# Moving the stationary buffers of the large products to 32 bytes past a 128-byte line

## The chip, the cores and the metric

The kernel runs on one core of one Trainium2 chip. The metric is device time in microseconds. Three runs of the kernel before took 1442.66, 1443.53 and 1445.46 us; the median is 1443.53.

## What is computed

A two-layer encoder trunk over 256 tokens of width 1024, all in float32:

```
h = x
hn = rms_norm(h, norm_mix[0]);  h += fourier_mixer(hn, w_in, w_out)        # h @ w_in, 2-D DFT by 4 groups, real part, @ w_out
hn = rms_norm(h, norm_ffn[0]);  h += (silu(hn @ w_gate) * (hn @ w_up)) @ w_down      # width 2816
hn = rms_norm(h, norm_mix[1]);  h += neighbourhood_attention(hn, w_qkv, rpb, w_o)    # 16 heads, 4 x 64 grid
hn = rms_norm(h, norm_ffn[1]);  h += moe_swiglu(hn, ...)                   # 8 experts of width 3584, the best 2 by token
out = rms_norm(h, final_norm)
```

Every expert's three matrices (1024 x 3584 twice, 3584 x 1024) are used, whatever the routing is, so all weights are read once: 423 MB in all.

## The kernel before

**The weight stream.** All large weight matrices are cut into pieces of 128 partitions x 2048 float32, 1 MB each: 4 row tiles x 512 columns for gate, up and projections, 2 row tiles x 1024 columns for down. SyncE loads them in order into seven buffers, `raw0` to `raw6` (L293). Each piece is then split in two, since a product in full float32 would be slow: ScalarE copies it to `w_hi` in the type float32r (L365), and VectorE writes the rest, `w_lo = raw - w_hi` (L624). There are three `w_hi` and three `w_lo` buffers. TensorE waits for `lo_made`, uses the piece, and its last matmul raises `piece_used`, on which ScalarE waits before it refills that buffer three pieces later. VectorE's `lo_made` frees the raw buffer for the next load.

**The large products.** The activations are split in the same way. The helper `three` (L995 to L997) issues three matmuls for one 128 x 128 block of activations and one row tile of weights:

```
nc.tensor.matmul(out_, xh, wh, start=start, stop=False)   # L995
nc.tensor.matmul(out_, xh, wl, start=False, stop=False)   # L996
return nc.tensor.matmul(out_, xl, wh, start=False, stop=stop)   # L997
```

The first operand, `xh` or `xl`, is the stationary one: 128 columns, loaded anew by an LDWEIGHTS ahead of each matmul. The second, `wh` or `wl`, is the moving one, 512 columns wide in nearly all cases. The stationary operand is `act_hi`/`act_lo` in the dense projections (w_in, w_out, gate, up, qkv, w_o; two blocks of 128 tokens), `hidT_hi`/`hidT_lo` in the down products of the dense layer and of the experts, and `xg_hi`/`xg_lo` in the gate and up products of the experts, whose tokens (at most 128) are gathered by a product with a selection matrix `sel` (L1299) and scattered back by `selT` (L1396, L1397). The Fourier mixer is made of products too: `u` by the table `dft` along the tokens (512 wide), then `dft` by `pt` along the channels (256 wide). In the profile's names the moving operand stands first: `bank_Y<-w_hi,hidT_hi` is moving `w_hi`, stationary `hidT_hi`.

**The order.** It is written out by hand, engine by engine. In an expert TensorE does, for each of 7 steps of 512 hidden columns, the gate product (2 pieces, 24 matmuls), the transposes of the step before (L1333), the up product (24) and the down product of the step before (24). Near the end of an expert come the gather for the next one and its transposes (L1310), then the last down products and the scatter. The 8 experts are a hardware loop with the same addresses each time.

**Where the buffers lie.** `sb(name, shape, dt)` in `trunk` allocates on-chip buffers one behind the other; each starts at the next multiple of 32 bytes. The order is `raw0` to `raw6`, `h`, `hn`, `gains`, `mask`, `act_hi`, `act_lo`, `ident`, some small ones, `silu_g`, `hid`, `hidT_hi`, `hidT_lo`, `arena`, `w_hi`, `w_lo`. The arena is one stretch in which four layouts lie over each other, one for each phase (Fourier, attention, experts, and the bias tables); `dft`, `u`, `pt`, `qT`, `kT`, `v`, `xg_hi`, `xg_lo`, `y_hi`, `y_lo`, `sel` and `selT` are in it. Three pads of 32 bytes, `pad_h`, `pad_g` and `pad_w`, stand ahead of `h`, `silu_g` and `w_hi`.

Of the kernel before, what the change touches and what calls it, by code (L numbers as in the profile page):

```python
# [26 lines left out]
P = 128  # L27
# [14 lines left out]
BANK = 512  # L42
PIECE = 2048
RAW = 7
SPLIT = 3
KH = PIECE // BANK
KROW = PIECE // D
# [58 lines left out]
PER_EXPERT = len(EXPERT)  # L106
assert PER_EXPERT % RAW == 0 and PER_EXPERT % SPLIT == 0


def expert_source(ewg, ewu, ewd, e, j):  # L110

    kind, c, half = EXPERT[j]
    v = {"gate": ewg, "up": ewu, "down": ewd}[kind][0].rearrange("e (k p) n -> p (e k) n", p=P)
    if kind == "down":
        return v[:, bass.ds(e * (FFE // P) + (BANK // P * c + KROW * half), KROW), :], KROW, D
    return v[:, bass.ds(e * KD + KH * half, KH), BANK * c:BANK * (c + 1)], KH, BANK


def trunk(nc, x, norm_mix, norm_ffn, w_in, w_out, w_qkv, w_o, ffg, ffu, ffd, router_w, router_b,
# [7 lines left out]
    N0 = len(dense)  # L127
    dense += [expert_source(ewg, ewu, ewd, 0, j) for j in range(SPLIT)]
    N1 = len(dense)


    def sb(name, shape, dt=f32):
        return nc.alloc_sbuf_tensor(name, shape, dt)

    raw = [sb(f"raw{i}", [P, PIECE]) for i in range(RAW)]
    sb("pad_h", [P, 8])
    h = sb("h", [P, NB, D])
    hn = sb("hn", [P, NB, D])
    gains = sb("gains", [P, 4, KD])
    mask = sb("mask", [P, GRID])  # L140
    act_hi = sb("act_hi", [P, KD, S], f32r)
    act_lo = sb("act_lo", [P, KD, S], f32r)
    ident = sb("ident", [P, P])
    sumsq = sb("sumsq", [P, 5, NB])
    rstd = sb("rstd", [P, 5, NB])
    half_power = sb("half_power", [P, NB])
    sb("pad_g", [P, 8])
    silu_g = [sb(f"silu_g{i}", [P, BANK]) for i in range(2)]
    hid = [sb(f"hid{i}", [P, BANK]) for i in range(2)]
    hidT_start = -(-nc.sbuf_base // 32) * 32  # L150
# [3 lines left out]
    def width_of(shape):  # L154

        return -(-4 * int(np.prod(shape[1:])) // 32) * 32

    def layout(entries, off):

        made = {}  # L160
        for name, shape, dt in entries:
            made[name] = nc.alloc_sbuf_tensor_at(name, shape, dt, offset=off)
            off += width_of(shape)
        return made
# [16 lines left out]
             ("gap", [P, NB], f32), ("ratio", [P, NB], f32), ("den", [P, NB], f32), ("g1", [P, NB], f32),  # L181
             ("g2", [P, NB], f32), ("weight", [P, NB, NE], f32), ("slot", [P, NB, 2 * NE], f32),
             ("most", [P, 1], f32), ("flag", [P, 1], i32)]
    arena_start = -(-nc.sbuf_base // 32) * 32
    sizes = [sum(width_of(shape) for _, shape, _ in l) for l in (fourier_l, attn_l, moe_l, bias_l + bias_l)]
    sb("arena", [P, max(sizes) // 4])
    sb("pad_w", [P, 8])
    w_hi = [sb(f"w_hi{i}", [P, PIECE], f32r) for i in range(SPLIT)]
    w_lo = [sb(f"w_lo{i}", [P, PIECE], f32r) for i in range(SPLIT)]
    fo, mo = (layout(l, arena_start) for l in (fourier_l, moe_l))  # L190
# [18 lines left out]
    def sem(name):  # L209
        return nc.alloc_semaphore(name)  # L210


    raw_in = [sem(f"raw_in{i}") for i in range(RAW)]
    hi_made, lo_made, piece_used, part_made = sem("hi_made"), sem("lo_made"), sem("piece_used"), sem("part_made")
# [35 lines left out]
    def piece(j, E, back=0):  # L250

        return j + 1 - back if E is None else E * PER_EXPERT + (N0 + j + 1 - back)

    def slot_of(j, E, n):
        return (j if E is None else N0 + j) % n

    def has_before(j, E, back):

        return E is not None or j >= back
# [28 lines left out]
    def _(sp):  # L288
        def load(j, E, src, tiles):
            s = slot_of(j, E, RAW)  # L290
            if has_before(j, E, RAW):
                sp.wait_ge(lo_made, piece(j, E, RAW))
            sp.dma_start(raw[s][:].rearrange("p (k n) -> p k n", k=tiles), src).then_inc(raw_in[s], 16)  # L293
# [9 lines left out]
        def expert_loads(E):  # L303

            for j in range(SPLIT, PER_EXPERT + SPLIT):
                e = E % NE if j < PER_EXPERT else (E + 1) % NE
# [49 lines left out]
    def _(act):  # L356
        made = [0]

        def split_hi(j, E):
            s, w = slot_of(j, E, RAW), slot_of(j, E, SPLIT)  # L360
            rounds = 16 * (j // RAW + 1) if E is None else 16 * ((N0 + j) // RAW + 1) + E * (16 * PER_EXPERT // RAW)
            act.wait_ge(raw_in[s], rounds)
            if has_before(j, E, SPLIT):
                act.wait_ge(piece_used, piece(j, E, SPLIT))
            nc.scalar.activation(w_hi[w][:], raw[s][:], ACT.Copy).then_inc(hi_made, 1)  # L365
# [1095 lines left out]
```

## Time and profile before

| | |
|---|---|
| median of three runs | 1443.53 us (1442.66 to 1445.46) |
| the profiled execution | 1442.99 us; span of its instructions 1441.1 us |
| TensorE matmul busy | 1398.6 us, 97% of the span, 6483 matmuls |
| VectorE busy | 1137.7 us, 79% |
| ScalarE busy | 944.7 us, 66% |
| GpSimd busy | 20.7 us, 1% |
| DMA | 423.16 MB, mean 294 GB/s |
| granted TensorE clock | 0.993 of full speed, mean over the span |

The dense part takes the first 335 us, attention and routing the next 90, and the eight experts some 1000 us, 125 us each. Matmuls are pipelined, so the records of two neighbours overlap: one of 512 columns is recorded with 0.39 us, while the next begins about 0.23 us after it. The distance between the starts tells the rate, the recorded duration doesn't.

### The profile page before, as it was taken

The page shows a single profiled execution, that of the slowest core. Times are in us where ns is not written, and L with a number is a line of the kernel's source. Part 1 is how long each engine was busy: PE and PEld are TensorE (multiplying, and loading weights), DVE is VectorE, ACT ScalarE, POOL GpSimd, SP SyncE. Part 2 cuts the span into 40 slices and gives each one's busy share as a digit, 9 for nine tenths or more (in the row PEclk, how much of TensorE's full clock was granted, in tenths as well). Part 3 has the DMA queues.
Part 4 walks back from the last instruction along what each step waited for, and adds up shares of the span by engine and source line. Part 5 has one row for each costly group of instructions (what it writes and reads, how often), then busy time and mean ns, then how long its engine had stood idle before and what let it go on. Part 6 is the DMA issues. An engine that isn't in the chain of part 4 may idle for free.

```text
span 1441.1 us, 17938 instructions
## 1 busy us (share of the span) xinstructions
PE 1398.6 (97%) x6483; PEld 1146.4 (80%) x6483; DVE 1137.7 (79%) x814; ACT 944.7 (66%) x773; POOL 20.7 (1%) x26
## 2 busy tenths in 40 slices
PE   6999999999979999999999999999999999999995
PEld 5888888787868887887888788788878878887884
DVE  5455666655578889888888988898898888889887
ACT  5354344445657777777777777777777777777775
POOL 0000000000120000000000000000000000000001
PEclk9999999999999999999999999999999999999998
DMA  9358775562149998998999899899989989999992
GB/s 356 106 170 225 215 207 176 175 205 88 59 135 340 371 377 304 373 369 311 367 378 355 318 370 369 315 362 365 370 307 381 363 321 372 357 353 332 368 375 85
DMA packets 192979, 423.16 MB, mean 294 GB/s; under 512 B 19184, under 2 KB 21360, under 8 KB 192944
## 3 DMA queue, kind: packets, MB, share of 16 engines
q1 hardware_dynamic: 179728, 418.15, 80.7%
q10 hardware_dynamic: 12784, 3.26, 1.6%
q0 software_dynamic: 432, 1.28, 0.3%
q8 instruction: 22, 0.36, 0.1%
q14 instruction: 13, 0.11, 0.0%
HBM read 421.61 MB, written 1.05 MB: 293 GB/s over the span
## 4 chain that ended last, share of the span: by engine, by line
PE 91%; DVE 3%; ACT 2%; issue 2%; POOL 0%; DMA 0%; ACTq 0%; DVEq 0%; POOLq 0%
PE bank_G L995 10%; PE bank_G L997 10%; PE bank_G L996 10%; PE bank_U L995 9%; PE bank_U L997 9%; PE bank_U L996 9%; PE bank_Y L995 8%; PE bank_Y L997 8%; PE bank_Y L996 8%; PE bank_T L1333 2%; DVE w_lo L624 1%; PE bank_G L1230 1%; PE bank_T L995 1%; PE bank_T L996 1%; PE bank_T L997 1%
## 5 line engine op out<-in xcount | busy, mean ns | idle before, releaser
L624 DVE TENSOR_TENSOR w_lo<-raw,w_hi 128x2048 fp32r<-128x2048 f32 x394 | 896.4, 2290 | 210.5 <-ACT w_hi L365 209.7
L365 ACT ACTIVATE w_hi<-raw 128x2048 fp32r<-128x2048 f32 x394 | 754.6, 1918 | 290.7 <-PE bank_U L997 93.3
L995 PE MATMUL bank_Y<-w_hi,hidT_hi 128*128 128x512 f32 x492 | 194.3, 395 | 0.0
L997 PE MATMUL bank_Y<-w_hi,hidT_lo 128*128 128x512 f32 x492 | 192.5, 391 | 0.0
L996 PE MATMUL bank_Y<-w_lo,hidT_hi 128*128 128x512 f32 x492 | 192.1, 390 | 0.0
L995 PE MATMUL bank_U<-w_hi,xg_hi 128*128 128x512 f32 x448 | 181.3, 405 | 0.5
L995 PE MATMUL bank_G<-w_hi,xg_hi 128*128 128x512 f32 x448 | 177.3, 396 | 1.4 <-DVE w_lo L624 0.5
L997 PE MATMUL bank_G<-w_hi,xg_lo 128*128 128x512 f32 x448 | 175.8, 392 | 0.0
L997 PE MATMUL bank_U<-w_hi,xg_lo 128*128 128x512 f32 x448 | 175.7, 392 | 0.0
L996 PE MATMUL bank_U<-w_lo,xg_hi 128*128 128x512 f32 x448 | 174.2, 389 | 0.0
L996 PE MATMUL bank_G<-w_lo,xg_hi 128*128 128x512 f32 x448 | 174.1, 389 | 0.0
L997 PEld LDWEIGHTS bank_Y<-w_hi,hidT_lo 128*128 128x128 f32 x492 | 92.4, 188 | 21.3
L996 PEld LDWEIGHTS bank_Y<-w_lo,hidT_hi 128*128 128x128 f32 x492 | 92.4, 188 | 19.8
L995 PEld LDWEIGHTS bank_Y<-w_hi,hidT_hi 128*128 128x128 f32 x492 | 92.5, 188 | 19.2
L995 PEld LDWEIGHTS bank_G<-w_hi,xg_hi 128*128 128x128 f32 x448 | 84.2, 188 | 21.7 <-DVE w_lo L624 4.7
L997 PEld LDWEIGHTS bank_G<-w_hi,xg_lo 128*128 128x128 f32 x448 | 84.1, 188 | 19.6
L997 PEld LDWEIGHTS bank_U<-w_hi,xg_lo 128*128 128x128 f32 x448 | 84.1, 188 | 19.5
L996 PEld LDWEIGHTS bank_G<-w_lo,xg_hi 128*128 128x128 f32 x448 | 84.1, 188 | 18.4
L995 PEld LDWEIGHTS bank_U<-w_hi,xg_hi 128*128 128x128 f32 x448 | 84.3, 188 | 17.2 <-DVE w_lo L624 2.1
L996 PEld LDWEIGHTS bank_U<-w_lo,xg_hi 128*128 128x128 f32 x448 | 84.3, 188 | 16.5
L995 PE MATMUL bank_G<-w_hi,act_hi 128*128 128x512 f32 (+1 forms) x176 | 68.2, 388 | 6.6 <-DVE w_lo L632 4.2
L995 PE MATMUL bank_U<-w_hi,act_hi 128*128 128x512 f32 (+1 forms) x176 | 67.7, 385 | 0.0
(262 smaller groups left out, 1482.8 us busy)
## 6 DMA issues: line engine op xcount, KB each, us to landing
raw<-in_expert_w_gate SPq DMA_DIRECT2D x114, 1024.0 KB, 7.2
raw<-in_expert_w_up SPq DMA_DIRECT2D x113, 1024.0 KB, 7.2
raw<-in_expert_w_down SPq DMA_DIRECT2D x112, 1024.0 KB, 6.8
raw<-in_nat_w_qkv SPq DMA_DIRECT2D x12, 1024.0 KB, 5.0
raw<-in_ffn_w_gate SPq DMA_DIRECT2D x11, 1024.0 KB, 8.8
raw<-in_ffn_w_up SPq DMA_DIRECT2D x11, 1024.0 KB, 5.2
raw<-in_ffn_w_down SPq DMA_DIRECT2D x11, 1024.0 KB, 5.5
raw<-in_fourier_w_in SPq DMA_DIRECT2D x4, 1024.0 KB, 11.3
```

The source lines that it names most:

```text
L365: nc.scalar.activation(w_hi[w][:], raw[s][:], ACT.Copy).then_inc(hi_made, 1)
L624: nc.vector.tensor_tensor(w_lo[w][:], raw[s][:], w_hi[w][:].bitcast(f32), ALU.subtract).then_inc(lo_made, 1)
L995: nc.tensor.matmul(out_, xh, wh, start=start, stop=False)
L996: nc.tensor.matmul(out_, xh, wl, start=False, stop=False)
L997: return nc.tensor.matmul(out_, xl, wh, start=False, stop=stop)
L1230: last = nc.tensor.matmul(G[i % 2][:, S * n:S * (n + 1)], att["qT"][p0:p0 + HD, m, P * b:P * (b + 1)], att["kT"][p0:p0 + HD, m, :], start= ...
L1333: last = nc.tensor.transpose(T[c % 2][:, P * k:P * (k + 1)], hid[c % 2][:, P * k:P * (k + 1)], ident[:])
```

## The change

The three fixed pads become computed ones, and two more are asked for. `past_line(name, 32)` allocates just what is missing for the next buffer to start 32 bytes past a multiple of 128, and nothing where it does so already. Nothing else is changed: no instruction, no wait, no order.

```diff
 RAW = 7
+LINE = 128
...
+    def past_line(name, bytes_past):
+        base = -(-nc.sbuf_base // 32) * 32
+        if (bytes_past - base) % LINE:
+            sb(name, [P, (bytes_past - base) % LINE // 4])
+
     raw = [sb(f"raw{i}", [P, PIECE]) for i in range(RAW)]
-    sb("pad_h", [P, 8])
+    past_line("pad_h", 32)
     h = sb("h", [P, NB, D])
...
     mask = sb("mask", [P, GRID])
+    past_line("pad_act", 32)
     act_hi = sb("act_hi", [P, KD, S], f32r)
...
-    sb("pad_g", [P, 8])
+    past_line("pad_g", 32)
     silu_g = [sb(f"silu_g{i}", [P, BANK]) for i in range(2)]
...
+    past_line("pad_a", 32)
     arena_start = -(-nc.sbuf_base // 32) * 32
...
     sb("arena", [P, max(sizes) // 4])
-    sb("pad_w", [P, 8])
+    past_line("pad_w", 32)
     w_hi = [sb(f"w_hi{i}", [P, PIECE], f32r) for i in range(SPLIT)]
```

## Rows read from the trace of the kernel before

**Rows 1.** The page, parts 1 and 4: TensorE's busy time; the chain by engine.
```profile
PE 1398.6 (97%) x6483; PEld 1146.4 (80%) x6483; DVE 1137.7 (79%) x814; ACT 944.7 (66%) x773; POOL 20.7 (1%) x26
PE 91%; DVE 3%; ACT 2%; issue 2%; POOL 0%; DMA 0%; ACTq 0%; DVEq 0%; POOLq 0%
```

**Rows 2.** By stage: us, busy PE, PEld, DVE, ACT, POOL, clock, DMA share, GB/s.
```profile
85.00:150.00 65.00, 65.00 (x297) 53.90 (x296) 36.84 (x28) 31.70 (x28) 0.92 (x2) 1.00 0.71 202
...
675.00:800.00 125.00, 124.26 (x560) 101.36 (x559) 109.84 (x69) 92.39 (x64) 0.00 (x0) 1.00 0.97 353
```

**Rows 3.** TensorE's timeline, dense up product: start us, us; first and last of 48.
```profile
96.63 0.39 PE L995 MATMUL bank_U<-w_hi,act_hi 128*128 128x512 f32 x1
...
107.28 0.39 PE L997 MATMUL bank_U<-w_hi,act_lo 128*128 128x512 f32 x1
```

**Rows 4.** TensorE's timeline, dense down product: first and last of 48.
```profile
130.17 0.39 PE L995 MATMUL bank_Y<-w_hi,hidT_hi 128*128 128x512 f32 x1
...
140.93 0.39 PE L997 MATMUL bank_T<-w_hi,hidT_lo 128*128 128x512 f32 x1
```

**Rows 5.** TensorE's timeline, expert: down product, then gate; first and last of 48.
```profile
574.61 0.39 PE L995 MATMUL bank_Y<-w_hi,hidT_hi 128*128 128x512 f32 x1
...
585.37 0.40 PE L997 MATMUL bank_G<-w_hi,xg_lo 128*128 128x512 f32 x1
```

**Rows 6.** Groups by line and form: xcount, busy us, mean ns, idle before.
```profile
L995 PE MATMUL bank_Y<-w_hi,hidT_hi 128*128 128x512 f32 x492 | 194.3, 395 | 0.0
L995 PE MATMUL bank_U<-w_hi,xg_hi 128*128 128x512 f32 x448 | 181.3, 405 | 0.5
L995 PE MATMUL bank_G<-w_hi,xg_hi 128*128 128x512 f32 x448 | 177.3, 396 | 1.4 <-DVE w_lo L624 0.5 <-DVE xg_lo L643 0.2
...
L995 PE MATMUL bank_G<-w_hi,act_hi 128*128 128x512 f32 x160 | 63.7, 398 | 6.6 <-DVE w_lo L632 4.2 <-DVE act_lo L647 1.4 <-DVE act_lo L643 0.9
...
L995 PE MATMUL bank_T<-w_hi,hidT_hi 128*128 128x512 f32 x40 | 15.8, 394 | 0.0
```

**Rows 7.** TensorE's timeline, expert, just behind the gather: first and last of 12.
```profile
661.09 0.40 PE L995 MATMUL bank_Y<-w_hi,hidT_hi 128*128 128x512 f32 x1
...
663.65 0.40 PE L997 MATMUL bank_Y<-w_hi,hidT_lo 128*128 128x512 f32 x1
```

**Rows 8.** The chain in order of time, start of an expert: start us, us, what.
```profile
682.07 1.10 issue
...
687.95 0.50 PE bank_G L995
```

**Rows 9.** TensorE's timeline, Fourier products: a run of 9, and a run of 24.
```profile
38.80 0.39 PE L995 MATMUL bank_T<-dft_hi,u_hi 128*128 128x512 f32 x1
...
40.61 0.39 PE L997 MATMUL bank_T<-dft_hi,u_lo 128*128 128x512 f32 x1
...
43.96 0.28 PE L995 MATMUL bank_Y<-pt_hi,dft_hi 128*128 128x256 f32 x1
...
46.72 0.28 PE L997 MATMUL bank_Y<-pt_hi,dft_lo 128*128 128x256 f32 x1
```

**Rows 10.** Groups by line and form, VectorE, the 128x512 rests.
```profile
L643 DVE TENSOR_TENSOR hidT_lo<-bank_T,hidT_hi 128x512 fp32r<-128x512 f32 x66 | 44.7, 683 | 3.6 <-ACT hidT_hi L459 3.6
...
L643 DVE TENSOR_TENSOR act_lo<-bank_G,act_hi 128x512 fp32r<-128x512 f32 x2 | 1.3, 686 | 2.2 <-ACT act_hi L491 2.2
```

**Rows 11.** Timelines of ScalarE and VectorE: one piece's split in an expert.
```profile
699.71 1.92 ACT L365 ACTIVATE w_hi<-raw 128x2048 fp32r<-128x2048 f32 x1 [0.82 <-PE bank_U L997]
...
701.73 2.29 DVE L624 TENSOR_TENSOR w_lo<-raw,w_hi 128x2048 fp32r<-128x2048 f32 x1
```

**Rows 12.** The tile raw: from the issue of a load to its landing.
```profile
DMA to landing us min/median/max: 4.7/7.0/16.7
```

**Rows 13.** TensorE's timeline: the first matmul of two experts, one after the other.
```profile
676.12 0.40 PE L995 MATMUL bank_G<-w_hi,xg_hi 128*128 128x512 f32 x1
...
801.01 0.40 PE L995 MATMUL bank_G<-w_hi,xg_hi 128*128 128x512 f32 x1
```

## The prediction

> **What bounds the kernel now.** I read the page's busy shares and the chain of waits first, then the table by stage, then the waits, and last the timeline of TensorE, row by row. The page has TensorE busy 97% of the span, and 91% of the chain that ended last is TensorE [rows 1]. The table by stage says the same of both halves: busy 65.00 of 65 us in a dense stretch and 124.26 of 125 us in an expert, at a granted clock of 1.00, which is the 2.4 GHz level [rows 2]. So the span is a count of matmuls times the distance between two starts; a busy time can't show that distance, since matmuls overlap in the records. It must be read as (last start minus first start) over the number of steps in a stretch without a gap.
>
> The kernel holds a natural experiment on exactly this. By the sizes in the program (a buffer starts at the next multiple of 32 bytes; the first is at 8320) act_hi and act_lo, w_hi and w_lo begin 32 bytes past a 128-byte line, while everything from silu_g to the arena's end begins 96 bytes past one: hidT_hi, hidT_lo, xg_hi, xg_lo, the gather's and scatter's operands, the Fourier operands.
> - Stationary act (32) with moving w (32): 48 matmuls in a row start between 96.63 and 107.28 us [rows 3], so 10.65/47 = 226.6 ns apart.
> - Stationary hidT (96), same moving buffers, a few us later at a like DMA load: 48 matmuls between 130.17 and 140.93 us [rows 4], 10.76/47 = 228.9 ns.
> - Expert phase, hidT and then xg (both 96): 48 matmuls between 574.61 and 585.37 us [rows 5], again 228.9 ns.
>
> The difference is 2.3 ns a matmul, it sets in with the first matmul on hidT without any wait between, and it is the same for two bank pairs, two tile families and two DMA loads. What those slow stretches have in common, and the fast one hasn't, is the place of the stationary operand.
>
> **The change, part by part.** No instruction is added or removed. Only addresses move.
> 1. pad_h: raw ends on a multiple of 128, so the computed pad is the same 32 bytes. The new pad_act comes out as none, since act_hi is at 32 already. h, hn, act, ident: nothing moves, cost 0.
> 2. pad_g grows from 32 to 96 bytes: silu_g, hid, hidT_hi, hidT_lo and the whole arena (xg, y, sel, selT, dft, u, pt, q, k, v) move up 64 bytes, from 96 to 32 past the line. This is the part that can pay.
> 3. pad_a comes out as none; pad_w grows by 64 bytes to 96, so w_hi and w_lo move up 128 bytes in all: still 32 past a 128-byte line.
>
> The value of part 2. The w-matmuls on hidT and xg are three for each row of line 995: 492 + 448 + 448 + 40 = 1428 rows, so 4284 matmuls [rows 6] (another four such rows are left out). If they step at the pace of rows 3, they save 4284 × 2.34 ns = 10.0 us. Bounds: nothing, if the place isn't the cause; and a little more, since after the gather of each expert a stretch runs at (663.65 - 661.09)/11 = 232.7 ns [rows 7] on the same hidT, and it might come down as well (some 20 matmuls in each of 8 experts, 6 ns: 1.0 us).
>
> What is not on the path. In each expert, right after the first gate product, PE waits for a piece that ACT was late with: between 682.07 and 687.95 us the chain runs through the table load, silu, w_hi and w_lo, not through the 24 matmuls of the first up product, which are issued meanwhile [rows 8]. Those 24 finish 0.06 us earlier and PE waits that much longer: 8 × 24 × 2.3 ns = 0.4 us, taken off.
>
> Gather (72), scatter (64) and Fourier token products (48) also move from 96 to 32, both operands at once. Their starts are unsteady, near 232 ns; at 226.6 the 184 would save 0.9 us, at unchanged pace nothing. I take 0, as they follow stalls or other shapes, and keep 0.9 for the range. The 256-wide products of the channel transform ran 24 matmuls from 43.96 to 46.72 us, 120 ns apart [rows 9]; the dense 256-wide ones on act are alike, so nothing is expected there. The 128-wide transposes, scores and p·v products have no pair to compare and are put at nothing either way.
>
> ACT and DVE also read and write moved tiles. Each 128x512 rest on DVE took 683 ns for hidT_lo at 96 and 686 ns for act_lo at 32 [rows 10]: no difference, and the large split (2290 ns) keeps its places in the line. They follow PE in any case.
>
> What could be late next. A piece takes 12 matmuls. ACT begins to refill a freed buffer at 699.71 us and DVE ends its half at 701.73 + 2.29 = 704.02 [rows 11]; PE wants it two pieces after it was freed, at about 705.2. At 2.72 us a piece instead of 2.75 that margin of 1.2 us loses 0.06. The loads come 4.7 to 16.7 us after issue, with a median of 7.0 [rows 12], seven buffers turn over in about 19 us, and no wait of ACT on a load appears among the long waits. The DMA would have to move 353 × 124.9/123.7 = 356 GB/s [rows 2], and single slices of this trace already show up to 381. So the gain should come through whole: 10.0 - 0.4 = 9.6 us.
>
> The sum is made against the profiled execution, 1442.99 us (span 1441.1): it becomes 1433.4. The median of the runs shown is 0.5 above it, so I forecast 1434.0. An expert, from 676.12 to 801.01 us now 124.89 us [rows 13], should take 124.89 - 480 × 0.00234 = 123.8.
>
> **A rule that speaks against it.** The trace shows a cost at 96 that isn't there at 32 [rows 3, 4]. The Trainium skill, page "SBUF — State Buffer", section "Specifications (TRN2)", gives 16-byte cachelines and a penalty for each crossing. Both 32 and 96 are whole such lines, and all rows here are contiguous, so by that rule the place costs nothing and the sum is 0. The measured rows decide for the larger step, but they don't prove that the step is 128 bytes.
>
> **The rivals.**
> - *It isn't the place in the line.* act differs from hidT and xg in other ways: act_lo lies 8192 bytes behind act_hi, the others 4096; act is read every 1024 bytes along k, the others every 512. For this: the Fourier token products, both operands at 96, ran from 38.80 to 40.61 us in 8 steps of 226.3 ns [rows 9], the fast pace, and their u_lo lies 8192 behind u_hi; and hidT itself ran at two paces [rows 5, 7]. Against: later Fourier products with the same tiles were slow. Then nothing changes: 1443.5 us.
> - *It is the distance between the stationary and the moving operand.* That was 64 in the slow stretches and 0 in act's and in the Fourier ones; after the change it is 0 throughout. Same time as the forecast; it belongs to it, and explains rows 9 better.
> - *The line that counts is 256 bytes or more.* w_hi0 goes from 169504 to 169632, that is from byte 32 to byte 160 of 256, and act stays at 32. If a moving operand there costs what the worst steady stretch shows, 232.7 ns [rows 7], then 4284 × 3.8 ns + 1056 × 6.1 ns (act: 352 rows of line 995, 160 of them in bank G [rows 6], as many in U, 16 each in Y and T) = 16.3 + 6.4 = 22.7 us more: 1466. In its mild form only act falls back to 228.9: 1056 × 2.3 ns = 2.4 us, 1446. It decides as soon as the dense act stretches aren't at 226.6 any more. Against: nothing in the trace distinguishes 32 from 160 of 256.
> - *Another engine takes over.* By the margins above PE's pace would have to fall by 0.1 us a piece and more before ACT and DVE bind; if half the gain were lost so, 1439.
>
> **How the numbers follow.** About 0.2%, 2.9 us, is what a measurement of this kernel can tell from no change. Forecast: 0.72, own range 1431.5 to 1437 (upper end: one third of the matmuls keep their pace; lower end: gather, scatter, Fourier and the 232.7 stretches come down too). Nothing: 0.15. Half lost: 0.04. 256-byte line, mild 0.03, full 0.06. Faster is 0.72 + 0.04 = 0.76, same 0.15 + 0.03 = 0.18, slower 0.06. The range reaches from 1431.5 up past the no-change case, to 1444.5.
>
> **What would show it.** Right: in the timeline the products on hidT and xg start 226.6 ns apart as act's do; an expert takes 123.8 us; w_lo stays at 2290 ns and w_hi at 1918; the wait for w_lo after each expert's first up product grows by 0.06 us. Wrong: 228.9 ns still there with everything at 32 (then another property of these tiles is the cause), act's stretches no longer at 226.6 (then 256 counts), or the new pace there and the expert still at 124.9 (then PE is not what sets the end).

## The result, and the profile after

The changed kernel takes 1463.89 us (median of 4 runs, 1462.22 to 1464.13), the kernel before, run beside it, 1443.22 us (median of 4). The ratio is 1.0138, 95% interval 1.0124 to 1.0152: slower by 20.7 us, where 9.5 us less had been forecast. The time lies near the rival "the line that counts is 256 bytes or more" in its full form (1466), which had been given a chance of 0.06.

The page of the changed kernel, parts 1, 4 and 5, answers to [rows 1] (its lines stand 9 further down: L1004 to L1006 are the three large matmuls, L633 and L374 the split).

```profile
span 1460.4 us, 17938 instructions
PE 1418.9 (97%) x6483; PEld 1149.3 (79%) x6483; DVE 1139.7 (78%) x814; ACT 946.8 (65%) x773; POOL 20.8 (1%) x26
PE 92%; DVE 3%; ACT 2%; issue 2%; POOL 0%; DMA 0%; ACTq 0%; DVEq 0%; POOLq 0%
L633 DVE TENSOR_TENSOR w_lo<-raw,w_hi 128x2048 fp32r<-128x2048 f32 x394 | 898.3, 2290 | 223.3 <-ACT w_hi L374 222.3
L374 ACT ACTIVATE w_hi<-raw 128x2048 fp32r<-128x2048 f32 x394 | 756.7, 1923 | 303.1 <-PE bank_U L1006 98.4
```

TensorE carries the chain as before. The instructions of ScalarE and VectorE last practically as long as before (1923 ns against 1918, and 2290 as before), they only wait a little more for work that TensorE frees. So the time must be in the distance between matmuls. TensorE's timeline of the changed kernel: first and last of 48 matmuls in the dense up product [rows 3], the dense down product [rows 4], an expert's down and gate products [rows 5], and the first matmul of two experts one after the other [rows 13].

```profile
98.21 0.39 PE L1004 MATMUL bank_U<-w_hi,act_hi 128*128 128x512 f32 x1
...
109.13 0.40 PE L1006 MATMUL bank_U<-w_hi,act_lo 128*128 128x512 f32 x1
...
132.53 0.40 PE L1004 MATMUL bank_Y<-w_hi,hidT_hi 128*128 128x512 f32 x1
...
143.46 0.39 PE L1006 MATMUL bank_T<-w_hi,hidT_lo 128*128 128x512 f32 x1
...
583.30 0.39 PE L1004 MATMUL bank_Y<-w_hi,hidT_hi 128*128 128x512 f32 x1
...
594.22 0.39 PE L1006 MATMUL bank_G<-w_hi,xg_lo 128*128 128x512 f32 x1
...
686.11 0.39 PE L1004 MATMUL bank_G<-w_hi,xg_hi 128*128 128x512 f32 x1
...
812.58 0.40 PE L1004 MATMUL bank_G<-w_hi,xg_hi 128*128 128x512 f32 x1
```

On act 10.92/47 = 232.3 ns a matmul, where it was 226.6; on hidT 232.6 and in the expert 232.3, where it was 228.9. Even act's products, whose stationary buffer has not moved by a byte, are slower. The only operand that moved there is the moving one, w_hi and w_lo, by 128 bytes.

The changed pace accounts for the loss. An expert takes 126.47 us instead of 124.89, eight of them 12.6 us. In the dense part and attention 1056 matmuls on act lose 5.7 ns each and 264 on hidT 3.7 ns: 6.0 + 1.0 us. Together 19.6; the two spans are 19.3 us apart.

### The profile page after: what moved, and what is told of

Same layout as the page of the kernel before. It is cut to its first block, busy times and chain, and to the rows that moved or that the text cites. A ratio compares the mean times of both kernels' runs of the same rounds, so it can differ in the third digit from the quotient of the medians.

```text
span 1460.4 us, 17938 instructions
## 1 busy us (share of the span) xinstructions
PE 1418.9 (97%) x6483; PEld 1149.3 (79%) x6483; DVE 1139.7 (78%) x814; ACT 946.8 (65%) x773; POOL 20.8 (1%) x26
## 4 chain that ended last, share of the span: by engine, by line
PE 92%; DVE 3%; ACT 2%; issue 2%; POOL 0%; DMA 0%; ACTq 0%; DVEq 0%; POOLq 0%
PE bank_G L1004 10%; PE bank_G L1006 10%; PE bank_G L1005 10%; PE bank_U L1004 9%; PE bank_U L1006 9%; PE bank_U L1005 9%; PE bank_Y L1004 8%; PE bank_Y L1006 8%; PE bank_Y L1005 8%; PE bank_T L1342 2%; DVE w_lo L633 1%; PE bank_G L1239 1%; PE bank_T L1004 1%; PE bank_T L1005 1%; PE bank_T L1006 1%
## 5 line engine op out<-in xcount | busy, mean ns | idle before, releaser
L633 DVE TENSOR_TENSOR w_lo<-raw,w_hi 128x2048 fp32r<-128x2048 f32 x394 | 898.3, 2290 | 223.3 <-ACT w_hi L374 222.3
L374 ACT ACTIVATE w_hi<-raw 128x2048 fp32r<-128x2048 f32 x394 | 756.7, 1923 | 303.1 <-PE bank_U L1006 98.4
L1004 PE MATMUL bank_Y<-w_hi,hidT_hi 128*128 128x512 f32 x492 | 194.9, 396 | 0.0
L1006 PE MATMUL bank_Y<-w_hi,hidT_lo 128*128 128x512 f32 x492 | 194.2, 395 | 0.0
L1004 PE MATMUL bank_U<-w_hi,xg_hi 128*128 128x512 f32 x448 | 181.6, 405 | 0.2
L1004 PE MATMUL bank_G<-w_hi,xg_hi 128*128 128x512 f32 x448 | 177.6, 397 | 1.5 <-DVE xg_lo L652 0.5
L1006 PE MATMUL bank_U<-w_hi,xg_lo 128*128 128x512 f32 x448 | 176.9, 395 | 0.0
L1006 PE MATMUL bank_G<-w_hi,xg_lo 128*128 128x512 f32 x448 | 176.9, 395 | 0.0
L1006 PEld LDWEIGHTS bank_Y<-w_hi,hidT_lo 128*128 128x128 f32 x492 | 92.6, 188 | 21.7
L1004 PEld LDWEIGHTS bank_Y<-w_hi,hidT_hi 128*128 128x128 f32 x492 | 92.7, 188 | 21.2
L1004 PEld LDWEIGHTS bank_G<-w_hi,xg_hi 128*128 128x128 f32 x448 | 84.4, 188 | 24.6 <-DVE w_lo L633 4.5
L1006 PEld LDWEIGHTS bank_U<-w_hi,xg_lo 128*128 128x128 f32 x448 | 84.4, 188 | 19.8
L1006 PEld LDWEIGHTS bank_G<-w_hi,xg_lo 128*128 128x128 f32 x448 | 84.3, 188 | 19.7
L1004 PEld LDWEIGHTS bank_U<-w_hi,xg_hi 128*128 128x128 f32 x448 | 84.5, 189 | 19.0 <-DVE w_lo L633 1.8
L1004 PE MATMUL bank_G<-w_hi,act_hi 128*128 128x512 f32 (+1 forms) x176 | 69.1, 392 | 6.6 <-DVE w_lo L641 4.2
L1004 PE MATMUL bank_U<-w_hi,act_hi 128*128 128x512 f32 (+1 forms) x176 | 68.5, 389 | 0.0
```

The source lines that it names most:

```text
L633: nc.vector.tensor_tensor(w_lo[w][:], raw[s][:], w_hi[w][:].bitcast(f32), ALU.subtract).then_inc(lo_made, 1)
```

## The experiments

In all of them but e8_line256 a helper `place(name, off)` is added to the kernel before, with `LINE = 256`: it allocates what is missing for the next buffer to start at byte `off` of a 256-byte line. pad_h and pad_g stay as they were; the diffs shown here are shortened and leave the helper out. "Distance" is the start of the stationary buffer minus the start of the moving one, modulo 256. In the kernel before it was 0 for act (w_hi0 at 169504, act_hi at 82464, apart by 340 × 256) and 192 for hidT and xg; in the changed kernel it is 128 for all of them. Theory D: the distance sets the pace. Theory M: the moving operand's own place does. Third theory: the 64-byte shift of the stationary buffers did the harm. The paces below are worked out from first and last starts of a stretch as above, in stretches with a granted clock of 1.00; starts are printed to 0.01 us, so a pace over 48 matmuls is good to some 0.2 ns and one over 24 to 0.4. Where only one run of a kernel is given, its time has no interval.

**The 64-byte shift without the shift of w (e1_w32).**

```diff
+LINE = 256
+    place("pad_act", 32)
+    place("pad_hidT", 32)
+    place("pad_a", 32)
-    sb("pad_w", [P, 8])
+    place("pad_w", 32)
```

> As the changed kernel, but w_hi and w_lo 128 bytes further on, so that act, hidT, the arena and w all begin at byte 32 of a 256-byte line (the changed kernel has w at byte 160). If the 256-byte line is what counts, whether by the place of the moving operand alone or by its distance from the stationary one, all large products start 226.6 ns apart and the time is 1443.2 minus about 10 us, 1433. If the slowdown comes from the 64-byte shift of the stationary buffers, the pace stays at 232.4 ns and the time at 1464. If a 512-byte line counts (w is at byte 288 of 512 here), act's products stay slow too.

Measured: 1439.66 us against 1446.21 for the kernel before on that chip, ratio 0.9956 (0.9940 to 0.9973): faster than both kernels, but short of the 10 us expected. Its timeline: the dense up product on act, 48 matmuls; in an expert down then gate, 48; the up product behind the transposes, 23 of its 24; and the start of two experts.

```profile
97.44 0.39 PE L1005 MATMUL bank_U<-w_hi,act_hi 128*128 128x512 f32 x1
...
108.09 0.39 PE L1007 MATMUL bank_U<-w_hi,act_lo 128*128 128x512 f32 x1
...
592.73 0.39 PE L1005 MATMUL bank_Y<-w_hi,hidT_hi 128*128 128x512 f32 x1
...
603.38 0.40 PE L1007 MATMUL bank_G<-w_hi,xg_lo 128*128 128x512 f32 x1
...
604.29 0.40 PE L1006 MATMUL bank_U<-w_lo,xg_hi 128*128 128x512 f32 x1
...
609.33 0.39 PE L1007 MATMUL bank_U<-w_hi,xg_lo 128*128 128x512 f32 x1
...
676.76 0.40 PE L1005 MATMUL bank_G<-w_hi,xg_hi 128*128 128x512 f32 x1
...
800.93 0.40 PE L1005 MATMUL bank_G<-w_hi,xg_hi 128*128 128x512 f32 x1
```

The first two stretches are both at 10.65/47 = 226.6 ns, as hoped. So the shift of the stationary buffers is good by itself, the third theory falls, and what is left for the harm is the shift of w. (silu_g and hid, which are no operands of these products, lie 64 bytes away from their place in the changed kernel too; e8_line256 below has them moved as well, and is as fast.) Here act and w are 256 bytes times an odd number apart (w at 288 of 512), and act's products ran at 226.6 all the same, so 512 doesn't count. The gain is 6.5 us instead of 10, because the up product hasn't changed: (609.33 - 604.29)/22 = 229.1 ns. The same 23 matmuls in the kernel before:

```profile
603.19 0.40 PE L996 MATMUL bank_U<-w_lo,xg_hi 128*128 128x512 f32 x1
...
608.23 0.39 PE L997 MATMUL bank_U<-w_hi,xg_lo 128*128 128x512 f32 x1
```

Also 229.1. At distance 192 a product behind the transposes is at its steady pace at once; at distance 0 its starts are uneven at first (from 604.29 to 606.38 us, 9 steps of 232 ns) and only then near 226.6. All 56 up products of the experts do so: the first nine steps of the 23 matmuls take 231.7 ns on average and the rest 226.5, in the kernel before 229.5 and 228.8. An expert has 7 such products: 7 × 23 × 2.3 ns = 0.4 us that didn't come, and 124.17 us an expert is 0.4 above the 123.8 of the forecast.

**w moved alone (e2_w160_only).**

```diff
-    sb("pad_w", [P, 8])
+    place("pad_w", 160)
```

> The kernel before with only w_hi and w_lo moved by 128 bytes, to byte 160 of 256; act stays at 32, hidT and the arena at 224. Theory of the moving operand's own place: everything is slow, 232.4 ns on act, hidT and xg, 1464 us. Theory of the distance: act (distance 128) is at 232.4, while hidT and xg (distance 64 from the other side) have a pace not seen yet, between 226.6 and 232.4. If w is innocent: the times of before, 1443, with 226.6 and 228.9.

Measured: one run, 1465.20 us against 1446.21. First and last of 48, on act, on hidT, and on hidT then xg:

```profile
97.71 0.39 PE L1002 MATMUL bank_U<-w_hi,act_hi 128*128 128x512 f32 x1
...
108.63 0.40 PE L1004 MATMUL bank_U<-w_hi,act_lo 128*128 128x512 f32 x1
...
132.03 0.40 PE L1002 MATMUL bank_Y<-w_hi,hidT_hi 128*128 128x512 f32 x1
...
143.00 0.39 PE L1004 MATMUL bank_T<-w_hi,hidT_lo 128*128 128x512 f32 x1
...
583.17 0.39 PE L1002 MATMUL bank_Y<-w_hi,hidT_hi 128*128 128x512 f32 x1
...
594.13 0.39 PE L1004 MATMUL bank_G<-w_hi,xg_lo 128*128 128x512 f32 x1
```

232.3 ns on act (distance 128), 233.4 and 233.2 on hidT and xg (distance 64). The 128 bytes of w alone cost 19 us, in one run. M's 232.4 came for act and not quite for the others; that hidT's pace differs from act's speaks for D. But D's guess for distance 64, between 226.6 and 232.4, was missed too: 64 is dearer than 128. "If w is innocent" falls.

**Everything at byte 160 (e3_all160).**

```diff
+    place("pad_act", 160)
+    place("pad_hidT", 160)
+    place("pad_a", 160)
-    sb("pad_w", [P, 8])
+    place("pad_w", 160)
```

> act, hidT, the arena and w all at byte 160 of 256: the distance between stationary and moving operand is 0 everywhere, as it was for act in the kernel before, but each operand is where w is in the changed kernel. Theory of the distance: 226.6 ns on all large products, about 1433 us. Theory of the moving operand's own place: 232.4 ns, 1464 us.

Measured: one run, 1440.69 us against 1446.21.

```profile
96.69 0.39 PE L1005 MATMUL bank_U<-w_hi,act_hi 128*128 128x512 f32 x1
...
107.35 0.39 PE L1007 MATMUL bank_U<-w_hi,act_lo 128*128 128x512 f32 x1
...
593.95 0.39 PE L1005 MATMUL bank_Y<-w_hi,hidT_hi 128*128 128x512 f32 x1
...
604.60 0.40 PE L1007 MATMUL bank_G<-w_hi,xg_lo 128*128 128x512 f32 x1
```

226.8 and 226.6 ns. The moving operand is at byte 160 of 256, as in the changed kernel, and the pace is the fast one. Theory M falls; D stands. The time is some 7 us above the 1433 expected; this kernel too has the uneven starts behind the transposes (231.4 ns over the first nine steps, 226.7 behind them).

**The other distances (e4_stat_map, e5_stat_map2).** w at byte 32; act, hidT and arena at 96, 160, 0 in the one and at 64, 128, 192 in the other, by the same four `place` calls.

> w at byte 32 of 256 as before; act at 96, hidT at 160, the arena (xg) at 0. It gives the pace for three more distances: 64, 128 and 224. Theory of the distance: hidT at distance 128 runs at 232.4 ns, act and xg between 226.6 and 232.4. Theory of the moving operand's own place: act, hidT and xg all stay at or under the 228.9 ns of the kernel before, since w is where it was, and the time is 1430 to 1446 us.

> w at byte 32 of 256; act at 64, hidT at 128, the arena (xg) at 192: the three distances not seen so far, 32, 96 and 160. The distance theory says that only 0 is free of cost, and predicts 229 to 234 ns for each, 1445 to 1467 us. If the cost grew steadily with the distance from 0, 32 would be the cheapest, below 229.

Measured: one run each, 1466.41 us (before: 1446.21) and 1467.14 us (before: 1444.45). The first kernel, on act (first and last of 48), hidT (48) and xg (24); then the second kernel in the same way.

```profile
99.30 0.39 PE L1005 MATMUL bank_U<-w_hi,act_hi 128*128 128x512 f32 x1
...
110.27 0.39 PE L1007 MATMUL bank_U<-w_hi,act_lo 128*128 128x512 f32 x1
...
133.78 0.39 PE L1005 MATMUL bank_Y<-w_hi,hidT_hi 128*128 128x512 f32 x1
...
144.71 0.39 PE L1007 MATMUL bank_T<-w_hi,hidT_lo 128*128 128x512 f32 x1
...
590.90 0.39 PE L1005 MATMUL bank_G<-w_hi,xg_hi 128*128 128x512 f32 x1
...
596.26 0.39 PE L1007 MATMUL bank_G<-w_hi,xg_lo 128*128 128x512 f32 x1
```

```profile
98.33 0.40 PE L1005 MATMUL bank_U<-w_hi,act_hi 128*128 128x512 f32 x1
...
109.30 0.40 PE L1007 MATMUL bank_U<-w_hi,act_lo 128*128 128x512 f32 x1
...
132.79 0.40 PE L1005 MATMUL bank_Y<-w_hi,hidT_hi 128*128 128x512 f32 x1
...
143.81 0.39 PE L1007 MATMUL bank_T<-w_hi,hidT_lo 128*128 128x512 f32 x1
...
590.08 0.39 PE L1005 MATMUL bank_G<-w_hi,xg_hi 128*128 128x512 f32 x1
...
595.45 0.39 PE L1007 MATMUL bank_G<-w_hi,xg_lo 128*128 128x512 f32 x1
```

With the other kernels this fills the table:

| distance, bytes of 256 | ns a matmul | where |
|---|---|---|
| 0 | 226.6 to 226.8 | act before; act, and hidT then xg, with everything at 32, at 160 or at 0 (steady stretches) |
| 32 | 233.4 | act, second map |
| 64 | 233.4; 233.2 to 233.4 | act, first map (w at 32); hidT and xg with w alone at 160 |
| 96 | 234.5 | hidT, second map |
| 128 | 232.3 to 232.6 | all of the changed kernel; act with w alone at 160; hidT, first map |
| 160 | 233.5 | xg, second map |
| 192 | 228.9 | hidT and xg before |
| 224 | 233.0 | xg, first map |

Where a distance came up with other tiles, in other stages and with w at another place (0, 64 and 128), it gave the same pace within 0.3 ns. 32, 96, 160, 192 and 224 were seen with w at byte 32 alone, and all but 192 in one run and with one tile. 0 is the cheapest distance, 192 costs 2.3 ns more, the other six 5.7 to 7.9 ns more. The cost doesn't grow steadily from 0. The first map also speaks against M: w hadn't moved within its 256 bytes, M had 228.9 or less, and 232.6 to 233.4 came. D had only 0 free of cost, and hidT at 232.4, which came; its ranges for the sizes were too low (act and xg under 232.4 in the first map; 229 to 234 in the second, where 234.5 came). So D is shown for what it says, that the pace goes with the distance, and it predicts no size.

**What the traces say of the 256-wide products.** The table above is for 512 columns. The dense projections also have products 256 columns wide, on act with moving w; 48 in a row, in the kernel before (distance 0) and in the first map (distance 64), first and last, in both at a granted clock of 1.00:

```profile
242.12 0.28 PE L995 MATMUL bank_G<-w_hi,act_hi 128*128 128x256 f32 x1
...
247.75 0.28 PE L997 MATMUL bank_G<-w_hi,act_lo 128*128 128x256 f32 x1
```

```profile
248.23 0.28 PE L1005 MATMUL bank_G<-w_hi,act_hi 128*128 128x256 f32 x1
...
253.77 0.28 PE L1007 MATMUL bank_G<-w_hi,act_lo 128*128 128x256 f32 x1
```

That is 119.8 ns and 117.9 ns. The same 48 took 120.0 ns each in the changed kernel (distance 128), 118.7 with w alone at 160 (128 too) and 118.3 in the second map (32). So the loss of 5.7 ns and more is one of the 512-wide products; the 256-wide ones lose nothing out of line, and are rather a little faster.

**One buffer of four out of line (e6_wlo160, e7_lo_pair160).**

```diff
     w_hi = [sb(f"w_hi{i}", [P, PIECE], f32r) for i in range(SPLIT)]
+    place("pad_w_lo", 160)
     w_lo = [sb(f"w_lo{i}", [P, PIECE], f32r) for i in range(SPLIT)]
```

The second kernel has this and the like in front of act_lo, hidT_lo and xg_lo; both have all else at 32.

> All stationary buffers and w_hi at byte 32 of 256, w_lo alone at 160: one of the three matmuls of each group (the one whose moving operand is w_lo) is at distance 128 from everything. Distance theory, by matmul: that one costs 5.7 ns more, the mean is 226.7 + 5.7/3 = 228.6 ns and the time 1439.7 + 5400 x 1.9 ns = 1450 us. If one distant buffer disturbs the whole stream: 232.4 ns and 1464 us.

> As the one before, and also act_lo, hidT_lo and xg_lo at byte 160; all hi buffers at 32. It tells with which stationary operand the moving one must agree. With its own: the matmuls hi x w_lo and lo x w_hi are both at distance 128, the mean is 226.7 + 2 x 5.7/3 = 230.5 ns, about 1460 us. With the next one, which is loaded while it streams: w_lo streams while lo is loaded (160 and 160), w_hi streams while hi is loaded (32 and 32), so all are at distance 0, 226.7 ns and 1440 us.

Measured: one run each, 1463.58 and 1456.88 us (before: 1444.45). First and last of 48, on act and on hidT then xg for w_lo alone, and then on act for the pair:

```profile
98.39 0.40 PE L1006 MATMUL bank_U<-w_hi,act_hi 128*128 128x512 f32 x1
...
109.36 0.39 PE L1008 MATMUL bank_U<-w_hi,act_lo 128*128 128x512 f32 x1
...
583.75 0.40 PE L1006 MATMUL bank_Y<-w_hi,hidT_hi 128*128 128x512 f32 x1
...
594.72 0.40 PE L1008 MATMUL bank_G<-w_hi,xg_lo 128*128 128x512 f32 x1
```

```profile
97.65 0.40 PE L1008 MATMUL bank_U<-w_hi,act_hi 128*128 128x512 f32 x1
...
108.51 0.39 PE L1010 MATMUL bank_U<-w_hi,act_lo 128*128 128x512 f32 x1
```

With w_lo alone out of line these stretches are at 233.4 ns, not 228.6: the simple sum by matmul, which I had put down for theory D, is refuted. The other branch on record, one distant buffer that disturbs the whole stream (232.4 ns, 1464 us), is near what came. But the pace isn't the same throughout: over all large products of this trace it is 232.7 on average, and some stretches are faster with the same buffers at the same distances, such as an expert's gate product from 686.82 to 692.08 us, 24 matmuls at 228.7 ns. So in this kernel something besides the distances has a say.

With the pair it is 231.1 ns on act, and 231.3 on hidT then xg (582.63 to 593.50 us): neither the 226.7 of "the operand that is loaded next must agree" nor the 230.5 of "its own must agree". The latter is the nearer, but either rule gives 228.6 for w_lo alone, and so had failed there already. Fewer buffers in line with w_hi gave the better time, so it isn't a count of buffers out of line either. By which mechanism the distances slow the stream stays open.

**Where the pads end up (e8_line256, e9_all0).** The changed kernel with `LINE = 256`; and all four groups at byte 0.

```diff
-LINE = 128
+LINE = 256
```

> The changed kernel with its one constant LINE set to 256 instead of 128; all five pads then place their buffers at byte 32 of a 256-byte line, h, silu_g and hid too. Against the kernel with act, hidT, the arena and w alone placed so (0.9956 of before) it adds h, hn, silu_g and hid. If those matter only in transposes, whose pace did not depend on the place, the ratio is the same, 0.9945 to 0.997.

> act, hidT, the arena and w all at byte 0 of 256: no buffer begins 32 bytes past anything, but all distances are 0. Distance theory: the same 226.7 ns in steady stretches as with all at 32 or all at 160, and a ratio to before of 0.995 to 0.997. If 32 past a line has a merit of its own, it is slower than those, with 228.9 ns or more.

Measured: 1439.16 us against 1444.45, ratio 0.9960 (0.9946 to 0.9974); and 1439.23 against 1443.77, ratio 0.9965 (0.9952 to 0.9977). Both ratios are in the range expected. The second kernel's timeline, on act and on hidT then xg:

```profile
97.56 0.39 PE L1005 MATMUL bank_U<-w_hi,act_hi 128*128 128x512 f32 x1
...
108.21 0.39 PE L1007 MATMUL bank_U<-w_hi,act_lo 128*128 128x512 f32 x1
...
592.56 0.39 PE L1005 MATMUL bank_Y<-w_hi,hidT_hi 128*128 128x512 f32 x1
...
603.21 0.40 PE L1007 MATMUL bank_G<-w_hi,xg_lo 128*128 128x512 f32 x1
```

226.6 ns both. Nothing has to begin 32 bytes past anything; for the gain of 4.5 to 6.5 us it is enough that all four groups begin at the same byte of 256. The three kernels of this kind have intervals that overlap, so which of them is best can't be told.

## Why the prediction was wrong

- *What bounds the kernel*: right. TensorE's chain is 92% and the whole difference is in the distance between matmuls. No other engine took over.
- *Part 1* (pads that come out the same) and the costs put at nothing for ScalarE and VectorE: right: 1923 and 2290 ns, and the 128x512 rests of VectorE still 683 and 686 ns.
- *Part 2* (64 bytes, worth 10.0 us): the sign was right and the pace of 226.6 ns came with w in line (e1_w32). The size was off: 6.5 us, since the up product behind each transpose stays near 229 ns. In the changed kernel none of it came.
- *Part 3* is the step that failed: "w_hi and w_lo move up 128 bytes in all: still 32 past a 128-byte line", with a cost of nothing. By itself it costs 19 us (e2_w160_only). It brought the distance to 128 everywhere, and the large products to 232.3 to 232.6 ns where 226.6 had been forecast. I had taken the 128 from the change's own constant. Nothing in the trace supported it: the fast pair of the kernel before was together modulo 128, 256 and 512 alike, so its rows couldn't tell one line from another. I said so under the third rival, and still gave it 0.09 in all.
- *The rival of the distance* named the right quantity and was filed with the forecast, because it was reckoned modulo 128: 64 for the slow stretches and 0 after the change. Modulo 256 it is 192 and 128, and then it doesn't belong to the forecast at all.
- *The rival of the 256-byte line* had the place, the sign and the price nearly right: 22.7 us forecast, 20.7 measured. It was priced with the pace of [rows 7], 232.7 ns, and 232.3 to 232.6 came. That the price fitted is luck: those rows stand behind the gather at distance 192, which runs at 228.9 when steady, so the pace there has another reason. The rival's own reason, the moving operand's own place, is refuted by e3_all160; the sign that it named, act's stretches no longer at 226.6, is what the trace shows.
- *The rival "it isn't the place in the line"*, by which spacings within the tiles would make the difference, falls with e1_w32: hidT and xg kept their spacings and ran at act's 226.6 ns.
- *Two small workings* were off and decided nothing. The 184 gather, scatter and Fourier products going from 232 to 226.6 would save 1.0 us, not 0.9. And the margin of 1.2 us over two pieces gives 0.6 us a piece before ScalarE and VectorE bind, where the fourth rival has 0.1.
- *The rule on cachelines*: the Trainium skill, page "SBUF — State Buffer", section "Specifications (TRN2)", has 16-byte lines. All starts in these kernels are multiples of 32 and the paces run from 226.6 to 234.5 ns, so the runs show an effect that this rule doesn't cover. That page's rule pointed to a sum of 0, which didn't come either.

## What to carry to other kernels

When matmuls reload the stationary operand each time, the start-to-start distance in an unbroken stretch is the number to watch. For products like these (float32r, 128x128 stationary, 512 columns moving) let the stationary and the moving buffers start at the same byte of a 256-byte line; which byte doesn't matter, and w_lo alone out of line cost nearly as much as everything. With 256 columns there was nothing to gain. If a rule on alignment is read from one fast pair, work out how far apart the pair is modulo several powers of two, before believing the smallest; a pad that keeps a small remainder can break a larger one, for buffers that nobody meant to touch. A pad computed for one purpose should be checked on everything allocated behind it.

## What the runs showed of the hardware that I had not expected

- The pace of a stream of 512-column products in float32r depends on the distance between its two SBUF operands modulo 256 bytes: 226.6 ns at 0, 228.9 at 192, 232.3 to 234.5 at the others tried, at a granted clock of 1.00. Over the kernel that is 1439 to 1467 us. Products of 256 columns don't lose by it (117.9 to 120.0 ns at distances 0, 32, 64 and 128). The Trainium skill, page "SBUF — State Buffer", section "Who interferes with whom", gives TensorE two independent read ports, one for the moving operand and one for LDWEIGHTS; the recorded LDWEIGHTS didn't get longer (188 to 189 ns), but the stream of both slowed down. By the runs the two reads are not without effect on each other.
- All Fourier operands lie in the arena and move together, so their distance is 0 in every kernel. The 512-wide Fourier products at the fast pace [rows 9], which the prediction counted for the rival "it isn't the place in the line", are what the distance gives.
- Behind the four transposes of a step a stream at distance 0 takes some ten matmuls to settle at its pace, 232 ns meanwhile (e1_w32, and much the same in the other three kernels with all at one byte); that is why aligned buffers gave 6.5 us and not 10.
